# Expert loop of two transformer stacks: two of three fp32r product groups put into one 512-column matmul, their halves added by ScalarE and VectorE

## Reference, cut to what matters

```python
def one_chunk(args):
    hc, ec, gc = args
    act = jax.nn.gelu(jnp.einsum('td,ted->te', hc, u[ec]).astype(f32), approximate=False)
    return jnp.einsum('te,ted->td', (gc * act).astype(v.dtype), v[ec])
```

## Time and profile before

| | |
|---|---|
| time, median of 3 executions | 3531.47 us (3530.13 to 3538.19) |
| span of the profiled execution | 3528.6 us |
| PE busy in the span | 3419.6 us, 97% |
| DVE busy | 2454.6 us, 70% |
| ACT busy | 1629.3 us, 46% |
| expert loop, layer 0 | 1817 to 2453 us of the span |
| expert loop, layer 1 | its last L1433 matmul starts at 3504.9 us |

### The profile page before, as it was taken

The page is one execution under the profiler, slowest core; times in us unless marked ns, Lnnn a source line. Parts: engine busy times, 40 slices in busy tenths (PEclk is TensorE's granted clock), DMA queues, the critical chain, the costliest instruction groups (busy, mean ns, idle before and its releaser), DMA issues.

```text
span 3528.6 us, 69418 instructions
## 1 busy us (share of the span) xinstructions
PE 3419.6 (97%) x24762; PEld 3075.1 (87%) x24762; DVE 2454.6 (70%) x5088; ACT 1629.3 (46%) x3273; POOL 323.4 (9%) x438
## 2 busy tenths in 40 slices
PE   8999999999999999999999999999899999999998
PEld 7879899988888998889888888888789888888887
DVE  6734456665435756547998888887447998888887
ACT  4143355434434643145555555554345555555554
POOL 0212000020210000000550000000000550000000
PEclk9999999999999999999999999999999999999999
DMA  7633478764336875134348778777254348787775
GB/s 219 182 90 97 116 220 262 229 189 120 84 95 184 262 236 129 49 104 144 92 122 195 193 191 192 190 192 172 63 147 143 91 128 193 190 194 191 192 192 134
DMA packets 644022, 565.20 MB, mean 160 GB/s; under 512 B 62027, under 2 KB 589402, under 8 KB 643546
## 3 DMA queue, kind: packets, MB, share of 16 engines
q1 hardware_dynamic: 638564, 542.16, 58.4%
q0 software_dynamic: 4960, 19.93, 1.7%
q10 hardware_dynamic: 278, 0.08, 0.0%
HBM read 550.52 MB, written 9.44 MB: 159 GB/s over the span
## 4 chain that ended last, share of the span: by engine, by line
PE 90%; DVE 4%; ACT 2%; DMA 1%; issue 1%; POOL 0%; SPq 0%; DVEq 0%; ACTq 0%; POOLq 0%
PE bank L1433 16%; PE bank L870 14%; PE bank L848 14%; PE bank L1453 7%; PE bank L1447 7%; PE bank L1450 7%; PE bank L891 4%; PE bank L1410 3%; PE bank L1385 3%; PE bank L844 2%; PE bank L1395 2%; PE bank L1364 1%; PE bank L1244 1%; PE bank L915 1%; PE bank L959 1%
## 5 line engine op out<-in xcount | busy, mean ns | idle before, releaser
L1433 PE MATMUL bank<-t_high,u_parts 128*128 128x256 f32 x3072 | 431.7, 283 | 5.1 <-DVE u_parts L3278 5.1
L1433 PEld LDWEIGHTS bank<-t_high,u_parts 128*128 128x128 f32 x3072 | 398.4, 188 | 43.3 <-issue 22.4
L3299 DVE TENSOR_TENSOR v_low<-ring,v_high 128x512 fp32r<-128x512 f32 x512 | 337.0, 689 | 62.9 <-ACT v_high L2167 38.3
L1453 PE MATMUL bank<-v_low,w_high 128*128 128x512 f32 x1024 | 323.2, 397 | 0.0
L1447 PE MATMUL bank<-v_high,w_high 128*128 128x512 f32 x1024 | 318.6, 392 | 0.0
L2167 ACT ACTIVATE v_high<-ring 128x512 fp32r<-128x512 f32 x512 | 299.3, 620 | 41.5 <-PE bank L1453 41.5
L1450 PE MATMUL bank<-v_high,w_low 128*128 128x512 f32 x1024 | 315.9, 390 | 0.0
L2370 POOL TENSOR_SCALAR uT<-cst,selT 128x128 f32<-128x128 f32 x256 | 188.2, 744 | 1352.2 <-ACT selT L2092 1347.8
L1726 ACT ACTIVATE arena<-bank 128x256 f32<-128x256 f32 (+1 forms) x270 | 103.8, 387 | 446.4 <-PE bank L848 249.6
L2155 ACT ACTIVATE u_parts<-bank 128x512 fp32r<-128x512 f32 x384 | 217.7, 593 | 194.8 <-DVE bank L3271 193.1
L848 PE MATMUL bank<-hT,ring 128*128 128x256 f32 (+2 forms) x1232 | 283.1, 387 | 9.4 <-DVE hT L2587 5.9
(11 more groups left out here) (455 smaller groups left out, 6434.0 us busy)
## 6 DMA issues: line engine op xcount, KB each, us to landing
ring<-in_peer_v SPq DMA_DIRECT2D x256, 512.0 KB, 4.6
ring<-in_peer_u SPq DMA_DIRECT2D x768, 128.0 KB, 4.3
ring<-in_w_in SPq DMA_DIRECT2D x128, 512.0 KB, 4.0
ring<-in_mlp_up SPq DMA_DIRECT2D x64, 512.0 KB, 4.3
uT<-in_mod_w SPq DMA_DIRECT2D x64, 512.0 KB, 4.9
ring<-in_mlp_down SPq DMA_DIRECT2D x64, 512.0 KB, 4.1
ring<-in_peer_u SPq DMA_DIRECT2D x64, 512.0 KB, 3.8
arena<-in_mod_w POOLq DMA_DIRECT2D x32, 512.0 KB, 4.9
```

What stands on the lines that cost most here:

```text
L1433: ins = eng.matmul(PB[6 + b][:, 0:S], u_parts[:, part, k * P:k * P + P], moving[:, k, :], start=(n == 0), stop=(n == len(products) - 1))
L1453: ins = eng.matmul(PB[2 * tt + q][:, :], w_high[:, b, t], v_low[:, j % 4, d], start=False, stop=last)
L3299: tt_(v_low[:, j % 4, d], ring[:, 2 + j % 4, d], v_high[:, d].bitcast(F32), ALU.subtract).then_inc(sem("vL_ready"), 1)
```

## The change

`score` now makes, for each of the eight k, one matmul of 512 columns of high rows: 256 columns of `t_low` and 256 of `t_high` (`turned_both(k)`, one access pattern over both places, for which both are views of one tensor). They fill both halves of the bank. Then come eight matmuls of 256 columns, low rows by `t_high`, added into the first half. The first eight need only `u_high`; the last eight wait for `u_low`, in two steps. ScalarE copies the second half of the bank into `gelu` (new `score_half`), VectorE adds the first half to it in place (new `score_sum`), and ScalarE takes Gelu of `gelu` in place. `score_half` stands on ScalarE ahead of `u_high` of the next tile, `score_sum` on VectorE ahead of `u_low` of the next tile. The bank is taken as free for a later score once `score_sum` is done (before: `gelu_done`).

```diff
--- before.py
+++ after.py
@@ -195,6 +195,21 @@
             t = nc.alloc_sbuf_tensor_at(name, shape, F32R, offset=address[over] + 4 * first)
             return t[(slice(None),) * len(shape)]
 
+        def spanning(name, *places):
+
+            at = [address[over] + 4 * first for over, first, _ in places]
+            base = min(at)
+            end = max(a + 4 * n * S for a, (_, _, n) in zip(at, places))
+            whole = nc.alloc_sbuf_tensor_at(name, [P, (end - base) // 4], F32R, offset=base)
+            first = [(a - base) // 4 for a in at]
+            return [whole[:, f:f + n * S].rearrange("p (k s) -> p k s", s=S) for f, (_, _, n) in zip(first, places)]
+
+        def pairs(one, other):
+
+            apart = other.offset - one.offset
+            return lambda i: bass.AP(one.tensor, (one if apart > 0 else other).offset + S * i,
+                                     [list(one.ap[0]), [abs(apart), 2], [1, S]])
+
         arena = sb("arena", [P, 32768])
         ring = sb("ring", [P, RING, 1024])
         xT = sb("xT", [P, KD, S])
@@ -220,9 +235,14 @@
         h_turned = ring[:, 6:8, :].rearrange("p b (k s) -> p (b k) s", s=S)
         less = rounded("less", "less_plain", 0, [P, P])
         h_low = rounded("h_low", "hT", 0, [P, KD, S])
-        t_high, t_low = rounded("t_high", "hT", 0, [P, KD, S]), rounded("t_low", "ring", 6 * 1024, [P, KD, S])
+        t_high, t_low = spanning("turned_parts", ("hT", 0, KD), ("ring", 6 * 1024, KD))
+        turned_both = pairs(t_low, t_high)
 
         PB = [ctx.enter_context(nc.psum_tensor(f"bank{i}", [P, 512], F32)) for i in range(8)]
+
+        def halves(bank):
+
+            return PB[bank][:, 0:2 * S].rearrange("p (a b) -> p a b", b=S)
 
         def C(name):
             at, n = CONST_AT[name]
@@ -1423,15 +1443,22 @@
 
                 def score(i, f):
                     b = f % 2
-                    eng.wait_ge(sem("uL_ready"), i * 12 + (2 * f + 2 + 2 * lbase))
-                    if positive(i * 6 + (f + fbase - 1)):
-                        eng.wait_ge(sem("gelu_done"), i * 6 + (f + fbase - 1))
-                    products = [(part, moving, k) for part, moving in ((1, t_high), (0, t_low), (0, t_high)) for k in range(KD)]
-                    for n, (part, moving, k) in enumerate(products):
-                        if isinstance(i, int) and i == 0 and f == 0 and n < 2 * KD and k % 2 == 0:
-                            eng.wait_ge(sem("h_split" if moving is t_low else "hH_ready"), H_PARTS * l + k // 2 + 1)
-                        ins = eng.matmul(PB[6 + b][:, 0:S], u_parts[:, part, k * P:k * P + P], moving[:, k, :],
-                                         start=(n == 0), stop=(n == len(products) - 1))
+                    eng.wait_ge(sem("uH_ready"), i * 12 + (2 * f + 2 + 2 * fbase))
+                    opening = isinstance(i, int) and i == 0
+                    if opening and f < 2:
+                        eng.wait_ge(sem("gelu_done"), f + fbase - 1)
+                    else:
+                        eng.wait_ge(sem("score_sum"), i * 6 + (f - 1 + lbase))
+                    for k in range(KD):
+                        if opening and f == 0 and k % 2 == 0:
+                            eng.wait_ge(sem("h_split"), H_PARTS * l + k // 2 + 1)
+                        eng.matmul(halves(6 + b), u_parts[:, 0, k * P:k * P + P], turned_both(k), start=(k == 0),
+                                   stop=(k == KD - 1))
+                    for k in range(KD):
+                        if k % 4 == 0:
+                            eng.wait_ge(sem("uL_ready"), i * 12 + (2 * f + 1 + k // 4 + 2 * lbase))
+                        ins = eng.matmul(PB[6 + b][:, 0:S], u_parts[:, 1, k * P:k * P + P], t_high[:, k, :], start=False,
+                                         stop=(k == KD - 1), skip_group_check=True)
                     ins.then_inc(sem("exp_mm"), 1)
 
                 def combine(i, j, first=False, last=False):
@@ -2169,11 +2196,10 @@
                 def activate(i, j):
                     b = j % 2
                     if j in FULL_AT:
-                        eng.wait_ge(sem("exp_mm"), i * 6 + (FULL_AT[j] + 1 + fbase))
+                        eng.wait_ge(sem("score_sum"), i * 6 + (FULL_AT[j] + 1 + FULL * l))
+                        eng.activation(gelu[:, b, :], gelu[:, b, :], ACT.Gelu).then_inc(sem("gelu_done"), 1)
                     if positive(i * 16 + (2 * j - 2 + 2 * base)):
                         eng.wait_ge(sem("v_free"), i * 16 + (2 * j - 2 + 2 * base))
-                    if j in FULL_AT:
-                        eng.activation(gelu[:, b, :], PB[6 + FULL_AT[j] % 2][:, 0:S], ACT.Gelu).then_inc(sem("gelu_done"), 1)
                     eng.wait_ge(sem("weighed"), i * 8 + (j + 1 + base))
                     eng.activation(w_high[:, b, :], gelu[:, b, :], ACT.Copy).then_inc(sem("wH_ready"), 1)
                     if not (isinstance(i, int) and i == 0 and j == 0):
@@ -2181,11 +2207,20 @@
 
                 def eight(i):
                     for j in range(8):
+                        if j in FULL_AT:
+                            score_half(i, j)
                         if j + 1 in FULL_AT and not (isinstance(i, int) and i == 0 and j == 0):
                             eng.wait_ge(sem("exp_mm"), i * 6 + (FULL_AT[j + 1] + fbase))
                             for q in range(2):
                                 u_high(l, i, FULL_AT[j + 1], q)
                         activate(i, j)
+
+                def score_half(i, j):
+                    f, b = FULL_AT[j], j % 2
+                    eng.wait_ge(sem("exp_mm"), i * 6 + (f + 1 + fbase))
+                    if positive(i * 8 + (j - 1 + base)):
+                        eng.wait_ge(sem("wL_ready"), i * 8 + (j - 1 + base))
+                    eng.activation(gelu[:, b, :], PB[6 + f % 2][:, S:2 * S], ACT.Copy).then_inc(sem("score_half"), 1)
 
                 eng.wait_ge(sem("exp_mm"), NKEY * l + EARLY)
                 turned_high(l, H_PARTS - 1)
@@ -3277,6 +3312,12 @@
                         eng.wait_ge(sem("uH_ready"), i * 12 + (2 * f + 2 * fbase + q + 1))
                         tt_(u_parts[:, 1, d], PB[4 + q][:, :], u_parts[:, 0, d].bitcast(F32), ALU.subtract).then_inc(sem("uL_ready"), 1)
 
+                def score_sum(i, j):
+                    f = FULL_AT[j]
+                    g = gelu[:, j % 2, :]
+                    eng.wait_ge(sem("score_half"), i * 6 + (f + 1 + FULL * l))
+                    tt_(g, g, PB[6 + f % 2][:, 0:S], ALU.add).then_inc(sem("score_sum"), 1)
+
                 def weigh(i, j):
                     b = j % 2
                     e = i * 8 + j
@@ -3301,6 +3342,8 @@
                 def eight(i):
                     for j in range(8):
                         f = FULL_AT.get(j + 1)
+                        if j in FULL_AT:
+                            score_sum(i, j)
                         if f is not None and not (isinstance(i, int) and i == 0 and f == 0):
                             u_low(i, f)
                         weigh(i, j)
```

## The result

The changed kernel takes 3560.92 us (median of 4, 3557.01 to 3568.63) beside 3530.80 us (median of 4) of the kernel before: a ratio of 1.0085, interval 1.007 to 1.010, so 0.85% slower, +30 us. I had forecast slower, by 64 us (3595 us, range 3575 to 3630). Measured later once more, the changed kernel was 32 us slower (3564.01 against 3532.17 us, ratio 1.0093, 1.0078 to 1.0109).

A forecast was written before the change was run, and what follows sets the result against it. PE bounds the kernel before, DVE's chain the changed one: 19.19 + 2 x 0.35 + 0.90 = 20.79 us a half against 19.78, +1.01 us in 64 halves, +64 us: 3595 us, range 3575 to 3630.

The forecast's parts named there:

- PE's work, 19.57 us, falling to 19.46: PE's matmuls in one half: three scores at 2.79 instead of 2.83 us, plus 11.08 us of combines.
- rival (d): Wide matmuls: the two-place operand is read slower; at 0.35 us each a half takes 22.3 us, 3692 us; chance 3%.
- The wait of 0.21 us for `u_low` goes: PE, start of each half's first score: the wait moves behind the eight wide matmuls, so 0.21 us goes.
- VectorE's chain as the next bound, with 0.60 us to absorb: DVE in the loop: needs 19.19 us a half beside PE's 19.57; only its 0.60 us wait for `v_high` is free.
- `score_sum` at 0.35 us of spacing: DVE, two of a half's three scored tiles: each addition costs 0.35 us start to start; bounds 0.33 and 0.5.
- its 0.43 us: DVE, each addition: the price if the next instruction waits for an empty pipe, 0.24 us more in a half.
- Third tile, 0.90 us: DVE, half's third scored tile: sum 0.42 plus Gelu round trip 0.48 us before `weigh`, paid in full; bounds 0.8 and 1.1.
- "PE follows", tightest at the first sum by 0.4 us: First sum of a half: `score_half` done 7.9 us after `weigh`, DVE there at 8.3, so no wait, by 0.4 us.
- Start of the loop, below 3 us: Once per layer the first score waits for the first `t_low` piece; below 3 us in all, counted as nothing.
- Rival (c): PE's granted clock falls in the loop because PE idles; at 0.8 a half takes 24.3 us, 3820 us; chance 2%.
- The chances: Whole kernel: slower 92%, within 0.2% 3%, faster 5%; some 85% for the range 3575 to 3630 us.

The follow-up runs named there:

- the run with the order alone: Kernel before with its 256-column matmuls in the changed kernel's order (rows' rests last), all summed in PSUM, no additions: 3521.47 us, ratio 0.9966.
- two repairs: Changed kernel with half of `v_low` moved behind `score_sum`: 3554.87 us; with wide matmuls and additions in the third tile only: 3556.88 us.

## Why the prediction was right or wrong, step by step

- *PE's work, 19.57 us, falling to 19.46:* right to 0.02 us: 19.56 with narrow matmuls, 19.48 with wide ones, so 27 ns a score where my rows gave 40. The two places of the operand cost nothing (0.233 us from start to start); rival (d) is out.
- *The wait of 0.21 us for `u_low` goes:* right, -12 us in the run with the order alone.
- *VectorE's chain as the next bound, with 0.60 us to absorb:* right in kind (DVE does bind the changed kernel), wrong in size. The step that failed is the one that took 19.79 - 0.60 = 19.19 us as DVE's own, with 1.38 us from transposes to `u_low` and 1.37 us to `weigh` in it as free of a wait, the latter since Gelu "had ended already". It had ended 0.13 us before; the run with the order alone shows 1.23 us where Gelu is earlier. The changed kernel shows 1.22 us at all three sums. The three gaps are 0.16 + 0.20 + 0.15 = 0.51 us a half and the split pair 0.09, together 0.60 us or 38 us in all; the third tile's round trip was 0.08 us longer than I had it, and the spacings of the other two sums 0.02 us shorter. That makes the 0.54 us by which the half was too long (20.79 against 20.25).
- *`score_sum` at 0.35 us of spacing:* right as a spacing (0.33 to 0.36), wrong as a price: 0.19 and 0.12 us in two of the three tiles, where the theory of the experiments had 0.17 each. The Trainium skill, "VectorE: DVE Perf Modes", section "The DRAIN you can't avoid", has the next instruction start only when the pipe is empty, but adds that one which is not held starts earlier; the prediction took only the first half of that for its 0.43 us. The rows of the changed kernel show such earlier starts: `u_low` started at 2008.29, 0.04 us before `score_sum`'s shown end, and at 2013.87 (2013.54 + 0.40) 0.07 us before it.
- *Third tile, 0.90 us:* the round trip was 0.98 us (2019.12 to 2020.10), since the wait for Gelu is 0.58 and not 0.48 us; against the 1.37 us of before it cost 1.22 + 0.98 - 1.37 = 0.83 us. Without this tile's additions the change is a gain (3519 us).
- *"PE follows", tightest at the first sum by 0.4 us:* right place, wrong size, by the same error. `score_half` was done 7.9 us after `weigh`, as forecast, but DVE came to the sum after 8.1 us and not 8.3; the room was 0.17 us, and 0.21 at the other two sums. It did not change this result, but it is what kept two repairs from working.
- *Start of the loop, below 3 us:* held in layer 0 for the scores, but it is not nothing: the second score started 1.3 us later than before (1825.83, not 1824.54). Layer 1 was not compared. The first score of layer 0 took 4.60 us instead of 3.69 (1816.85 to 1820.54), with the granted clock at 0.79 in its stretch, where the kernel before shows 1.00:

```profile
1818.00:1826.00 8.00, 7.59 (x29) 6.12 (x30) 7.49 (x14) 3.29 (x8) 0.00 (x0) 0.79 0.69 183
1826.00:1834.00 8.00, 8.00 (x43) 6.76 (x43) 5.92 (x11) 4.70 (x10) 0.00 (x0) 1.00 1.02 208
```
```profile
1818.41 3.09 PE L1455 MATMUL bank<-turned_parts,u_parts 128*128 128x512 f32 x8 [1.79 <-DVE turned_parts L3358]
1821.30 1.91 PE L1460 MATMUL bank<-turned_parts,u_parts 128*128 128x256 f32 x8
1823.01 0.66 PE L1474 MATMUL bank<-v_high,w_high 128*128 128x512 f32 x2
```

  Eight 256-column matmuls took 1.71 us there (1821.30 to 1823.01) instead of 0.94, after PE had waited 1.79 us for the input's rest and had been paced by it. From 1826 on the clock was 1.00, in layer 0 to the end of its loop; in layer 1 it was 0.92 at the start (2900 to 2910) and 1.00 in every 100 us from 3000 to 3500. Rival (c), a clock that falls in the loop because PE idles, is out.
- *The chances:* slower 92% was right. The range was too narrow below. Between no change and 3575 us I had left next to nothing, though the sum rested on a difference of 0.4 us between two chains of 19 us, and an error of 0.1 us in each of five links moves it by 32 us. The lower bound of each step behind the transposes should have been the 1.21 us after which other pairs of VectorE go on (`u_low`, 2021.86 to 2023.07).

## What to carry to other kernels

An idle time that a view does not print is not zero: in a chain of instructions each just ready in time, compare the start-to-start distance of a pair in the chain with the same pair where nothing gates it, and price an added instruction by what is left over. Of two edits in one change, look which one pays: here the order gives 12 us alone, the wide matmuls 5 to 10 more, and the additions that they need cost 51. Where an added step is a round trip to another engine, ask whether other work stands between its two ends; the same step cost 0.19 and 0.12 us in two tiles and 0.83 in the third.

## What was not expected of the hardware

DVE started its next instruction 0.04 to 0.09 us before the shown end of the one ahead, waits on semaphores between them included. The distance from an ACT instruction's shown end to the DVE instruction that waits for it was not one number: 0.03 us for `w_high` to `w_low` (2020.76 + 0.42, then 2021.21) and 0.12 us for Gelu to `weigh` (2019.56 + 0.42, then 2020.10) in the rows shown. `weigh` reads a column that is chosen by a loop register, and Gelu is another function than Copy; which of the two makes the 0.09 us was not tried.
